# Hybrid decoder block: C products on four column groups, index weights through the key tile, five tile copies to four trig steps

## What is computed

```
h = layer_norm(x)
proj = h @ w_in                      # u, q, k, v, q_idx, k_idx, w_idx (8 columns), gate_pre
# A) state space branch: 32 groups x 16 channels, 64 complex states a group
bu = einsum('blgp,gnp->blgn', u, b_bar)            # complex
states = associative_scan(a_bar, bu)               # over the 512 positions
y = einsum('blgn,gpn->blgp', states, c_c).real + d_skip * u
y_ssm = glu(gelu(y) @ w_glu)
# B) sparse attention: an index score picks 128 keys for each query
dots = einsum('bqhd,bsd->bhqs', q_idx, k_idx) * 64 ** -0.5
score = einsum('bqh,bhqs->bqs', w_idx * 8 ** -0.5, relu(dots))
sel = top_k(score, 128);  softmax attention on the chosen keys with distance penalties
mix = (sigmoid(gate) * (y_ssm, y_att)) @ w_o ;  h = layer_norm(alpha * h + mix)
h = layer_norm(alpha * h + moe(h))   # top 4 of 32 experts, clamped SwiGLU
```

## Time and profile before

| | us |
|---|---|
| median of 3 runs | 1830.73 |
| lowest, highest | 1827.61, 1830.94 |
| the profiled execution's own time | 1829.8 |
| its span, first to last instruction | 1828.0 |

### The profile page before, as it was taken

The page is one execution under the profiler, slowest core; times in us unless marked ns, Lnnn a source line. Parts: engine busy times, 40 slices in busy tenths (PEclk is TensorE's granted clock), DMA queues, the critical chain, the costliest instruction groups (busy, mean ns, idle before and its releaser), DMA issues.

```text
span 1828.0 us, 22681 instructions
## 1 busy us (share of the span) xinstructions
PE 1687.9 (92%) x7227; PEld 1138.0 (62%) x7227; DVE 1518.6 (83%) x1709; ACT 1082.1 (59%) x1032; POOL 526.0 (29%) x310
## 2 busy tenths in 40 slices
PE   3889989989997689999999999999999999999992
PEld 2333347667666357777777777777777777777761
DVE  6899927945376779999999999999999999999994
ACT  4332213355444257777777777777777777777770
POOL 4655114366062361221212122121212222121220
PEclk9999989998898589999999999999999999999996
DMA  6110121211123669999999999999999999999973
GB/s 194 46 46 2 45 92 46 70 69 47 70 66 115 220 242 355 364 368 366 376 360 365 369 368 365 363 378 355 364 371 369 364 361 382 360 364 366 381 270 106
DMA packets 93084, 465.44 MB, mean 255 GB/s; under 512 B 22404, under 2 KB 22520, under 8 KB 43800
## 3 DMA queue, kind: packets, MB, share of 16 engines
q1 hardware_dynamic: 81776, 443.90, 63.6%
q0 software_dynamic: 9424, 16.86, 4.0%
q10 hardware_dynamic: 1848, 4.24, 0.6%
HBM read 454.81 MB, written 18.92 MB: 259 GB/s over the span
## 4 chain that ended last, share of the span: by engine, by line
PE 79%; DVE 15%; ACT 2%; issue 2%; DMA 1%; POOL 1%; ACTq 0%; DVEq 0%; POOLq 0%
PE ps L1701 19%; PE ps L1703 19%; PE ps L1702 19%; PE ps L1687 3%; PE ps L1442 2%; PE ps L1437 2%; PE ps L1709 2%; PE ps L1423 2%; DVE scr L1113 1%; DVE top L1112 1%; PE ps L1431 1%; DVE scr L1063 1%; PE ps L1433 1%; PE ps L1432 1%; PE ps L1576 1%
## 5 line engine op out<-in xcount | busy, mean ns | idle before, releaser
L1191 DVE TENSOR_TENSOR w_lo<-raw,w_hi 128x2048 fp32r<-128x2048 f32 x384 | 874.4, 2288 | 81.8 <-ACT w_hi L847 81.8
L847 ACT ACTIVATE w_hi<-raw 128x2048 fp32r<-128x2048 f32 x384 | 737.0, 1920 | 242.1 <-PE ps L1703 242.1
L1701 PE MATMUL ps<-w_hi,x_hi 128*96 128x512 f32 x1024 | 414.8, 405 | 0.0
L1703 PE MATMUL ps<-w_lo,x_hi 128*96 128x512 f32 x1024 | 403.8, 394 | 0.0
L1702 PE MATMUL ps<-w_hi,x_lo 128*96 128x512 f32 x1024 | 403.4, 394 | 0.0
L625 POOL DMA_INDIRECT gate_now<-gate_rows,row_now x32 | 80.3, 2510 | 467.9 <-DVE tok_out L1319 447.5
L1703 PEld LDWEIGHTS ps<-w_lo,x_hi 128*96 128x96 f32 x1024 | 165.8, 162 | 71.3 <-issue 0.5
L1701 PEld LDWEIGHTS ps<-w_hi,x_hi 128*96 128x96 f32 x1024 | 168.6, 165 | 66.1 <-issue 0.5
L1701 PE MATMUL ps<-w_hi,a_hi 128*96 128x512 f32 x512 | 204.5, 399 | 5.7 <-DVE a_lo L1290 5.7
L1702 PEld LDWEIGHTS ps<-w_hi,x_lo 128*96 128x96 f32 x1024 | 166.3, 162 | 64.7 <-issue 0.3
L1702 PE MATMUL ps<-w_hi,a_lo 128*96 128x512 f32 x512 | 201.4, 393 | 0.0
(11 more groups left out here) (311 smaller groups left out, 2277.5 us busy)
## 6 DMA issues: line engine op xcount, KB each, us to landing
raw<-in_w_up SPq DMA_DIRECT2D x256, 1024.0 KB, 8.2
raw<-in_w_down SPq DMA_DIRECT2D x128, 1024.0 KB, 7.0
ring<-in_w_in SPq DMA_DIRECT2D x9, 2048.0 KB, 7.9
ring<-in_w_glu SPq DMA_DIRECT2D x4, 1024.0 KB, 6.2
ring<-in_w_o SPq DMA_DIRECT2D x2, 2048.0 KB, 13.0
h<-in_x SPq DMA_DIRECT2D x4, 512.0 KB, 4.8
ring<-in_w_attn_proj SPq DMA_DIRECT2D x1, 2048.0 KB, 7.9
h_rows<-h ACTq DMA_DIRECT2D x4, 512.0 KB
```

The lines of the kernel that those rows point to most:

```text
L847: s.activation(hi_of(c)[:, :], raw_of(c), ACT.Copy).then_inc(s_hi, 1)
L1191: d.tensor_tensor(lo_of(c)[:, :], raw_of(c), hi_of(c)[:, :], ALU.subtract).then_inc(s_lo, 1)
L1701: mm(o, xh, hi_of(c)[:, col], start=start, stop=False)
L1703: return mm(o, xh, lo_of(c)[:, col], start=False, stop=stop)
```

## The change

Five parts go together.

1. `ymm(q)` does four steps, 4q to 4q+3, on the four column groups of the array. There are five state buffers instead of three: the two new ones lie in `far` and in `gb`. So the load of the two rows ln_in_g and ln_in_b into `gb` moves from behind chunk 1 to behind chunk 8.
2. The index weights become eight further columns of the ki tile (72 rows of output). A new tile `wi`, behind the first q tile, turns rows 64 to 71 with four transposes; ScalarE takes it with the scale. Then SP copies rows 0 to 63 of the keys to rows 64 to 127 by DMA.
3. The narrow products, the second small load and VectorE's scaling go.
4. ScalarE takes tiles by the list `TAKEN_BY`: five between four trig steps.
5. TensorE's program places `bu` and `ymm` by two tables, `bu_at` and `y_at`, between the 21 tiles, with the last `ymm` behind the last tile.

```diff
-NSMALL = 136
+NSMALL = 72
...
-        w_st = [scr[:, 8:12], scr[:, 12:16], ring[:, 5, 1536:3584].rearrange("p (k t) -> p k t", k=4)]
+        w_st = [scr[:, 8:12], scr[:, 12:16], ring[:, 5, 1536:3584].rearrange("p (k t) -> p k t", k=4),
+                far[:, :, :], gb[:, :, :].rearrange("p r (k t) -> p (r k) t", k=2)]
...
-        for kind, n in (("u", 4), ("qi", 4), ("ki", 1), ("q", 4), ("k", 4), ("v", 4), ("g", 16)):
-            tiles += [(kind, i, "a") for i in range(n)]
+        for kind, lo, hi in (("u", 0, 4), ("qi", 0, 4), ("ki", 0, 1), ("q", 0, 1), ("wi", 0, 1), ("q", 1, 4), ("k", 0, 4),
+                             ("v", 0, 4), ("g", 0, 16)):
+            tiles += [(kind, i, "a") for i in range(lo, hi)]
...
-        tiles_upto = [4, 8, 13, 17, 21, 25, 29, 33, 37, 45, 53, 61]
+        tiles_upto = [4, 8, 14, 18, 22, 26, 30, 34, 38, 46, 54, 62]
...
-            sp.dma_start(small[:, :, 0:64], w_in[:, :, C_KI:C_KI + 64]).then_inc(s_small, 16)
-            sp.dma_start(small[:, :, 64:136], w_in[:, :, C_KI:C_KI + 72]).then_inc(s_small, 16)
+            sp.dma_start(small, w_in[:, :, C_KI:C_KI + 72]).then_inc(s_small, 16)
             for n in range(1, NFRONT):
                 chunk(n)
-                if n == 1:
+                if n == 3:
+                    sp.wait_ge(s_tile, first_tile["wi"] + 1)
+                    sp.dma_start(kiT[64:128, :], kiT[0:64, :]).then_inc(s_kdup, 16)
+                if n == 8:
+                    sp.wait_ge(s_stfree, SJ // 4)
                     for r, nm in enumerate(("ln_in_g", "ln_in_b")):
                         sp.dma_start(gb[:, r, :], a[nm].partition_broadcast(P)).then_inc(s_gb1, 16)
...
-            pool.wait_ge(s_wi, 1)
+            pool.wait_ge(s_tile, first_tile["g"])
...
-                    ins = s.activation(kiT[:, :], src[:, :], ACT.Copy)
+                    ins = s.activation(kiT[0:72, :], src[0:72, :], ACT.Copy)
+                elif kind == "wi":
+                    ins = s.activation(wi[:, :, :].rearrange("p t h -> p (t h)"), src[:, 0:TT * HEADS], ACT.Copy,
+                                       scale=HEADS ** -0.5)
...
+            TAKEN_BY = [1, 2, 3, 4, 5, 7, 8, 10, 11, 13, 14, 15, 16, 18, 19, 20]
             for j in range(SJ):
                 trigs(j)
-                take(n)
-                n += 1
+                while n <= TAKEN_BY[j]:
+                    take(n)
+                    n += 1
...
-                if j >= 3:
-                    dve.wait_ge(s_stfree, (j - 3) // 2 + 1)
-                w = w_st[j % 3]
+                if j >= 5:
+                    dve.wait_ge(s_stfree, (j - 5) // 4 + 1)
+                w = w_st[j % 5]
...
-            dve.wait_ge(s_wi, 1)
+            dve.wait_ge(s_tile, first_tile["g"])
             dve.wait_ge(s_hThi, 1)
...
-            step(d.tensor_scalar(wi[:, :, :], wi_ps(ps), HEADS ** -0.5, None, ALU.mult))
+            dve.wait_ge(s_tile_a, taken[first_tile["wi"]][1])
...
-                        ins = mm(o[:, :], small[:, k, 0:P], hT[:, k, :], start=k == 0, stop=k == KD - 1)
+                        ins = mm(o[0:72, :], small[:, k, :], hT[:, k, :], start=k == 0, stop=k == KD - 1)
+                elif kind == "wi":
+                    for t in range(TT):
+                        ins = tr(o[:, HEADS * t:HEADS * t + HEADS], kiT[64:72, P * t:P * t + P], ident[64:72, 64:72])
...
-                pe.wait_ge(s_st, 2 * p + 2)
-                if p % 2 == 0 and q > 1:
+                pe.wait_ge(s_st, 4 * q + 4)
+                if q > 1:
                     pe.wait_ge(s_yfree, q - 1)
                 for k, r in enumerate((0, 2, 1, 1)):
-                    for j in (2 * p, 2 * p + 1):
+                    for j in range(4 * q, 4 * q + 4):
...
-            order = [(0, 3), (1, 4), ("small", 1), (2, 4), (3, 4), (4, 4)]
+            order = [(0, 3), (1, 4), ("small", 1), (2, 1), ("wi", 1), (2, 3), (3, 4), (4, 4)]
             flat = [c for c, cnt in order for i in range(cnt)]
+            bu_at = {1: 1, 4: 2, 7: 3, 10: 4, 13: 5, 15: 6, 18: 7}
+            y_at = {6: 0, 12: 1, 17: 2}
...
-                if i % 2 == 0 and 1 <= i // 2 <= SJ // 2:
-                    ymm(i // 2 - 1)
-                if i % 2 == 1 and i // 2 + 1 < SJ // 2:
-                    bu(i // 2 + 1)
-
-            pe.wait_ge(s_bufree, SJ)
-            for t in range(TT):
-                for k in range(KD):
-                    ins = mm(ps[7][:, HEADS * t:HEADS * t + HEADS], hT[:, k, P * t:P * t + P], small[:, k, P:P + HEADS],
-                             start=k == 0, stop=k == KD - 1)
-            ins.then_inc(s_wi, 1)
+                if i in y_at:
+                    ymm(y_at[i])
+                if i in bu_at:
+                    bu(bu_at[i])
+
+            ymm(3)
...
             pe.wait_ge(*taken[n - 1])
+            pe.wait_ge(s_kdup, 16)
```

More of the change, by code:

```diff
@@ L261, in build @@
         s_w1o = sem("w_o_right_loaded")
-        s_wi = sem("w_idx_done")
+        s_kdup = sem("index_keys_copied")
         s_const = sem("pool_constants")
@@ L416, in _ @@
                     sp.dma_start(craw[:, r, :, 64 * dup:64 * dup + 64], src).then_inc(s_par[2], 16)
[L417 to L418 removed]
+            sp.dma_start(small, w_in[:, :, C_KI:C_KI + 72]).then_inc(s_small, 16)
             for n in range(1, NFRONT):
                 chunk(n)
[L421 removed]
+                if n == 3:
[3 more added lines that the diff above has]
+                    sp.wait_ge(s_stfree, SJ // 4)
                     for r, nm in enumerate(("ln_in_g", "ln_in_b")):
                         sp.dma_start(gb[:, r, :], a[nm].partition_broadcast(P)).then_inc(s_gb1, 16)
+                if n == 1:
                     sp.dma_start(w_rt[:, :, :], a["w_router"][0].rearrange("(k p) n -> p k n", p=P)).then_inc(s_par[3], 16)
@@ L771, in _ @@
             s.activation(hT_hi[:, :, :], hT, ACT.Copy).then_inc(s_hThi, 1)
-            act.wait_ge(s_stfree, SJ // 2)
+            act.wait_ge(s_stfree, SJ // 4)
             gate_hi(0)
@@ L1073, in y_out @@
             def y_out(q):
-                dve.wait_ge(s_stfree, 2 * q + 2)
+                dve.wait_ge(s_stfree, q + 1)
                 d.scalar_tensor_tensor(uT[:, q, :], uT[:, q, :], dskip[:, q:q + 1], ps[5 - q % 2][:, :],
@@ L1477, in bu, with ymm @@
                 ins.then_inc(s_bu, 1)
-            def ymm(p):
-                q = p // 2
-                pe.wait_ge(s_st, 2 * p + 2)
-                if p % 2 == 0 and q > 1:
+            def ymm(q):
+                pe.wait_ge(s_st, 4 * q + 4)
+                if q > 1:
                     pe.wait_ge(s_yfree, q - 1)
                 for k, r in enumerate((0, 2, 1, 1)):
-                    for j in (2 * p, 2 * p + 1):
+                    for j in range(4 * q, 4 * q + 4):
                         rows = slice(32 * (j % 4), 32 * (j % 4) + 32)
-                        ins = mm(ps[5 - q % 2][rows, :], cblk[:, r, j, :], w_st[j % 3][:, k, :], start=k == 0, stop=k == 3)
+                        ins = mm(ps[5 - q % 2][rows, :], cblk[:, r, j, :], w_st[j % 5][:, k, :], start=k == 0, stop=k == 3)
                 ins.then_inc(s_stfree, 1)
-            order = [(0, 3), (1, 4), ("small", 1), (2, 4), (3, 4), (4, 4)]
+            order = [(0, 3), (1, 4), ("small", 1), (2, 1), ("wi", 1), (2, 3), (3, 4), (4, 4)]
             flat = [c for c, cnt in order for i in range(cnt)]
+            bu_at = {1: 1, 4: 2, 7: 3, 10: 4, 13: 5, 15: 6, 18: 7}
+            y_at = {6: 0, 12: 1, 17: 2}
             bu(0)
@@ L1496, in _ @@
                 if c == "small":
-                    pe.wait_ge(s_small, 32)
-                elif c != (flat[i - 1] if i else 0):
+                    pe.wait_ge(s_small, 16)
+                elif c != "wi" and c != (flat[i - 1] if i else 0):
                     arrive(c)
-                tile(n, c if c != "small" else 0)
+                tile(n, c if c not in ("small", "wi") else 0)
                 n += 1
-                if i % 2 == 0 and 1 <= i // 2 <= SJ // 2:
-                    ymm(i // 2 - 1)
-                if i % 2 == 1 and i // 2 + 1 < SJ // 2:
-                    bu(i // 2 + 1)
-            pe.wait_ge(s_bufree, SJ)
-            for t in range(TT):
-                for k in range(KD):
-                    ins = mm(ps[7][:, HEADS * t:HEADS * t + HEADS], hT[:, k, P * t:P * t + P], small[:, k, P:P + HEADS],
-                             start=k == 0, stop=k == KD - 1)
-            ins.then_inc(s_wi, 1)
+                if i in y_at:
[3 more added lines that the diff above has]
+            ymm(3)
             def gate_tile(n):
```

2 lines of the change are left out of this document (removed).

## The result

| | before | after |
|---|---|---|
| median, runs made together (us) | 1830.2 (4 runs) | 1808.12 (4 runs) |
| lowest, highest | 1827.61, 1830.94 | 1807.61, 1809.26 |
| profiled execution, its span | 1829.8, 1828.0 | 1807.76, 1806.0 |
| VectorE's last step ends | 232.5 | 238.3 |
| first gate tile starts | 276.6 | 259.1 |

The ratio is 0.9883, 95% interval 0.9872 to 0.9895: faster by 1.2%. The forecast was 1813.0 with a range of 1804.5 to 1819.0.

The account below looks back on a forecast made before the run. TensorE's backlog behind VectorE's state space steps was taken to bound the start of the gate stage. Gate tile 258.9 plus the block of 1551.4 gave a span of 1810.2, execution 1812.0, median 1813.0 us; range 1804.5 to 1819.

Parts of the forecast that it names:

- C call on four steps: C products in the state space steps: one call on four steps takes 3.6 us; eight calls become four, 14.4 us less.
- B: C products: groups run two by two or weight loads laid bare, 7.1 us a call, about 1817.5 us; chance 0.12.
- C: C products: four groups run one after the other, 14.3 us a call, slower at 1846 us; chance 0.06.
- Transposes: Index weights on TensorE: four transposes of 8 rows take 0.5 us, plus a ScalarE copy of about 0.6 us.
- TensorE waits about 10 us in three places: State space steps: TensorE waits for VectorE to free input banks, 10.2 us, plus 3.4 us of low clock for one wait.
- (a): VectorE's state space steps: input products of call 7 come late, so VectorE waits 1.5 us.
- (b): VectorE's steps: VectorE and GpSimd hold each other up through phase work, 2.7 us more, bounds -3 and +6.
- rival A: Phase work falls no worse, clock does not drop before the last C call: 1805.5 to 1807 us; chance 0.14.
- Last C call at half rate: Behind VectorE's last step: TensorE's idle time brings the low clock, so the last C call takes 7.0 instead of 3.6 us.
- Tail: Serial chain behind the last C call, through distances, hT_hi, GpSimd's hT_lo and wg_lo, to first gate tile at 258.9 us.
- The same 1551.4 us behind: Everything behind the first gate tile moves as a block and keeps its 1551.4 us.
- Rival D: Attention stage's clock shifts and gives the gain back: within 4 us of before, or part lost; chance 0.06.

Follow-up runs that it names:

- the second profile: The changed kernel profiled once more, unchanged: 1808.41 us, ratio 0.9892 to the kernel before.
- filler: Changed kernel plus six unneeded 128x512 products in TensorE's idle time before the last C call: 1812.56 us, ratio 0.9908 to the kernel before.
- early_round: Changed kernel with ScalarE's hT_hi waiting only for the last C call, no longer for VectorE's distances: 1805.12 us, ratio 0.9872 to the kernel before.
- all_on_vector: early_round with all of hT_lo on VectorE and none on GpSimd: 1807.71 us, ratio 0.9886 to the kernel before.
- two_by_two: Changed kernel with the C products on two column groups at a time instead of four: 1811.29 us, ratio 0.9895 to the kernel before.

## Why the prediction held, step by step

The kernel got faster by the forecast chain, and the gate tile came where it was forecast. How close it came is luck: two terms were off and nearly cancelled (steps 5 to 7), and the second profile has it 2.0 us later. The time of 1808.1 lies in the stated range, but below the 1809 to 1816 that the forecast gave by its own terms (step 8).

1. **C call on four steps, 3.6 us:** 3.6. The Trainium skill, in "TensorE: Matmul & The Clock Gate", Part 3, has a list of what overlaps, by which a weight load overlaps only with products on other row groups, and gives three column groups 2.38 times the pace. (The text above that list also lets a load into the background weight buffer go ahead.) The trace disagrees with the list and the table: four groups here run at four times the pace, 0.43 us for a quadruple, with their loads of 0.11 us unseen. Rivals B and C fall by this row.
2. **Transposes 0.5 us, one more copy 0.6:** the four transposes are one row of 0.41 us, the copy 0.19.
3. **TensorE waits about 10 us in three places, the largest, 6 us, before input call 4:** the sum was right, 3.14 + 0.44 + 0.76 + 5.31 = 9.7. The place was not: the large wait came before call 6. The low clock came behind two of the waits, 3.14 and 5.31 us, where the sum had it once. The last tile ended at 232.7, forecast 231.3.
4. **(a) Call 7 late, VectorE waits 1.5 us:** it waited 4.81. This is the step that failed, and by its own rows. The 28.6 us had call 6 and the tile behind it at full clock. With the wait of 5.3 us before it, call 6 took 3.73 and the tile 8.74: 1.8 and 1.6 us more, and 1.5 + 3.4 = 4.9. I had charged that price once, at call 4, where VectorE wasn't waiting for it.
5. **(b) VectorE and GpSimd, 2.7 us more:** of the 5.8 us by which the last step ends later, 4.81 are (a), 0.2 a later start and 0.4 a longer wait before step 1. 0.4 is left for (b), and 0.7 in the second profile: the order put the phases hardly worse than before, which is what rival A had. In all the last step came 5.8 us later in place of 4.2, and 7.5 in the second profile.
6. **Last C call at half rate, 7.0 us:** 5.2. It ran at half rate for four of its eight quadruples, and then the clock was back. After 5.68 us without work the low clock did come, which rival A had not wanted; in filler, with the idle time filled, it did not come.
7. **Tail, first gate tile 258.9:** 259.1, and 260.9 in the second profile. Steps 5 and 6 nearly cancel, +1.6 and -1.8, and that is luck: in the second profile they are +3.3 and -1.6.
8. **The same 1551.4 us behind:** the sum gave a span of 1810.2 and it was 1806.0. The mis-sized term is this one: 1546.9, 4.5 us less. The change takes no work of TensorE away behind the gate tile; the profile of before that I summed against had an attention stage at a clock of 0.90, and the same kernel at 0.98 has a block of 1545.3. Its gate tile, at 276.6, was the earliest of three, and by the means above the gain at the gate is near 20, not 17.8. Rival D, a gain given back behind, holds neither for the changed kernel nor for early_round. It does describe filler and all_on_vector, as far as one profile of each goes.
9. **Slips in the sums:** the terms of the tail add up to 258.8 and those of A to 251.2, 0.1 and 0.2 less than written. B and C priced the last call lower than the rule of step 6 would: at half rate B's 7.1 us would be 14.2, and C's 14.3 would be 28.6. two_by_two measured 7.7. With 14.2, B would have come near 1821, above the 1819 at which the range ends.

The forecast's reasoning that only the late part of TensorE's relief counts is what the parts show: C products alone 0, index weights alone 8.8, both 8.6, C products with the takes 18.3, all three 21. The takes alone, and the takes with the index weights only, were not run, so what the C products in fours add to the takes is not known beyond the 2.5 us of two_by_two.

## What to carry to other kernels

When one engine is late, look for what admits its work before making its work shorter: here a copy on a third engine limited the tiles. 14 us less work earned nothing while the copies came one to a step; five to four steps, with the order that goes with them, earned 18 us on top of it. When a sum is made against one profiled run, profile the same kernel twice, since two of its terms moved by 3 and 6 us in opposite directions. The long waits on TensorE (3.1 to 5.7 us here) cost again in the operations right behind them, so charge that price to the path that each of them delays.

## What the runs showed of the hardware

- Column groups are independent in time: in two_by_two the second pair started 1.75 us into the first pair's 3.6, and four groups side by side cost what one does. Products of different groups did not start in the program's order (243.08 before 245.06).
- TensorE's low clock came after 3.1, 5.3 and 5.7 us without work (an input call of 3.78 or 3.73 us in place of 1.99, records of 1.06 in place of 0.59), and not after 0.76. It did not come before the last C call when the idle time there was filled.
- The clock in the attention stage was 0.90, 0.92, 0.94 or 0.98 for the same 513 records, 91.0 to 98.9 us of TensorE's time. In filler and all_on_vector a lower clock there stands beside the loss of a gain of 2 us made 100 us earlier; that the gain was the cause is not shown.
- A GpSimd operation of 2.4 us that started 1.0 us into a VectorE operation of 4.43 us was waited for until 2.3 us behind that one's end: as if it had done nothing until VectorE's was over.
